# One layer's tokens taken past attention in two chunks, the expert gather of the first issued while the second is still in dense work

## The reference, cut to what matters

```
h = rmsnorm(x, norm1_g) * (1 + sc1) + sh1
f_in, c_in, q/k/v ..., gl = split(h @ w_in)
y_f, y_c, y_a, y_w = four mixers, each @ its output weights
gates = sigmoid(gl + b_gate)
merged = g0 * y_f + g1 * y_c + g2 * y_a + g3 * y_w
x = x + g1 * (merged @ w_out)
h = rmsnorm(x, norm2_g) * (1 + sc2) + sh2
q = (h @ w_q) as 8 heads x 2 halves of 128;  scores = q . subkeys (128 keys)
per head: top 16 of each half -> 256 pairs -> top 16 pairs -> 16 expert numbers
act = gelu(u[e] . h);  x = x + g2 * sum over 128 slots (softmax gate * act) * v[e]
```

## Time and profile before

| | |
|---|---|
| runs | 6071.48, 6000.5, 6046.06 us |
| profiled execution | 6077.76 us, its span 6075.9 us |
| mean granted TensorE clock | 0.873 |
| busy share of the span | PE 78%, PEld 44%, DVE 59%, ACT 14%, POOL 26% |
| DMA | 1509.71 MB, of which 1342.26 MB by the indirect gathers |
| last chain by engine | PE 47%, DMA 37%, DVE 10%, ACT 3% |

### The profile page before, as it was taken

How to read it: one execution, slowest core, us unless ns; L and a number is a source line. 1 busy time by engine, 2 the same in 40 slices (tenths; PEclk the granted TensorE clock), 3 DMA queues, 4 the chain that set the end, 5 groups by cost and what they waited for, 6 DMA issues and landing times.

```text
span 6075.9 us, 45921 instructions
## 1 busy us (share of the span) xinstructions
PE 4730.4 (78%) x14848; PEld 2693.3 (44%) x14848; DVE 3560.2 (59%) x7774; ACT 849.0 (14%) x2368; POOL 1566.3 (26%) x1310
## 2 busy tenths in 40 slices
PE   5989999896666666666679899998966666666665
PEld 3766677762222222222248566777722222222222
DVE  0655211158888888876419333111488888888765
ACT  1023200101111111111011322001011111111111
POOL 0000000004444454445200000000044444454453
PEclk7989999998888888888799669999988888888887
DMA  5100011119999999999730000111099999999997
GB/s 233 56 28 1 30 59 64 49 47 422 420 408 421 407 421 412 422 420 421 315 151 28 28 1 22 63 60 58 28 389 421 410 421 413 421 412 421 421 421 291
DMA packets 213696, 1509.71 MB, mean 248 GB/s; under 512 B 24656, under 2 KB 26960, under 8 KB 37072
## 3 DMA queue, kind: packets, MB, share of 16 engines
q0 software_dynamic: 184320, 1342.26, 53.3%
q1 hardware_dynamic: 29136, 164.52, 7.4%
HBM read 1503.54 MB, written 3.15 MB: 248 GB/s over the span
## 4 chain that ended last, share of the span: by engine, by line
PE 47%; DMA 37%; DVE 10%; ACT 3%; issue 2%; POOL 1%; DVEq 1%; SPq 0%; POOLq 0%; ACTq 0%
DMA B<-tables,R 21%; PE ps L625 9%; DMA A<-tables,R 8%; PE ps L702 7%; DMA R<-tables,R 6%; PE ps L465 5%; PE ps L630 5%; PE ps L682 4%; DVE B L1234 3%; DVE hT L1266 3%; PE ps L450 2%; PE ps L644 2%; PE ps L562 2%; PE ps L549 2%; DMA B<-ws 2%
## 5 line engine op out<-in xcount | busy, mean ns | idle before, releaser
L702 PE MATMUL ps<-B,hT 128*128 128x512 f32 x2752 | 1593.7, 730 | 768.8 <-ACT hT L897 768.8
L392 POOL DMA_INDIRECT B<-tables,R x908 | 1098.2, 1209 | 2784.7 <-DVE A L1223 1599.1
L702 PEld LDWEIGHTS ps<-B,hT 128*128 128x128 f32 x2752 | 623.6, 234 | 1706.6 <-ACT hT L897 932.5
L1234 DVE SCALAR_TENSOR_TENSOR B<-B,M 128x1024 f32<-128x1024 f32 x908 | 1096.1, 1224 | 319.7 <-DMA B<-tables,R 294.6
L702 PE MATMUL ps<-A,hT 128*128 128x512 f32 x864 | 528.8, 748 | 265.8 <-ACT hT L897 265.8
L625 PE MATMUL ps<-hT,B 128*128 128x320 f32 x2048 | 561.9, 432 | 1.4 <-ACT R L856 1.4
L625 PEld LDWEIGHTS ps<-hT,B 128*128 128x128 f32 x2048 | 389.0, 190 | 164.9 <-ACT R L856 3.0
L702 PEld LDWEIGHTS ps<-A,hT 128*128 128x128 f32 x864 | 198.6, 239 | 570.7 <-ACT hT L897 323.5
L392 POOL DMA_INDIRECT A<-tables,R x272 | 334.2, 1229 | 350.6 <-PE ps L702 268.2
L891 ACT ACTIVATE T<-T 128x4 f32<-128x4 f32 x320 | 65.7, 205 | 2413.6 <-DVEq L1236 2413.6
L1234 DVE SCALAR_TENSOR_TENSOR A<-A,M 128x1024 f32<-128x1024 f32 x272 | 332.8, 1225 | 116.9 <-DMA A<-tables,R 108.0
(11 more groups left out here) (205 smaller groups left out, 4695.8 us busy)
## 6 DMA issues: line engine op xcount, KB each, us to landing
B<-ws SPq DMA_DIRECT2D x96, 1024.0 KB, 4.9
B<-ws SPq DMA_DIRECT2D x64, 768.0 KB, 4.1
B<-tables,R POOLq DMA_INDIRECT x908, 17.9
R<-tabs SPq DMA_DIRECT2D x2, 2176.0 KB, 8.3
A<-tables,R POOLq DMA_INDIRECT x272, 20.4
x<-xin SPq DMA_DIRECT2D x1, 2560.0 KB, 9.2
y<-M SPq DMA_DIRECT2D x1, 2560.0 KB, 7.9
R<-tables,R POOLq DMA_INDIRECT x100, 18.4
```

The source lines that it names most:

```text
L392: pool.indirect_dma_start(out=ring[HOME[n]], out_offset=None, in_=tables[:, :], in_offset=bass.IndirectOffsetOnAxis(ap=EI[:, n:n + 1], axi ...
L702: mm = pe.matmul(ps[:, bk + c, :], diag[p % DIAGS], v_row[:, c * 512:(c + 1) * 512], start=(gt == 0 and i == 0), stop=(gt == GROUPS - 1 an ...
L1234: v.scalar_tensor_tensor(out=u_row, in0=u_row, scalar=1.0, in1=h2[:, n // SLOTS, :], op0=ALU.mult, op1=ALU.mult, accum_out=dots[:, n % (2 ...
```

## The change

From the merge on, tokens go in two chunks: tiles 0 and 1 (256 tokens), then tiles 2, 3 and 4 (384). The first chunk goes through merge, output projection, norm, queries and the selection for tile 0 alone. Then TensorE, ScalarE and VectorE interleave the second chunk's merge, projection, norm and queries with the expert work of tiles 0 and 1, by a fixed list in each engine. Those tiles' slots go in groups of 2 (before: 4). Of the two sums of a group one is TensorE's and one VectorE's up to slot 163; from slot 164 to 255, which is from the second chunk's queries on, both are TensorE's. Tiles 2 to 4 keep groups of 4 with three sums on TensorE. All 44 weight blocks past attention are loaded a second time. The ring starts with 6 homes, has 7 from slot 132, 12 from slot 236 and at last 15. The sigmoid becomes a tanh of half the argument, with the factors of one half put into a bias and into the row that scales the residual. In the front of the layer, halves of 512 and 128 columns become 256 and 384.

```diff
+CHUNKS = ((0, 1), (2, 3, 4))
-RING = 10
-NG = 4
+RING = 6
+GROUPS = [Group(t, n, size, size if 164 <= n < 2 * SLOTS else size // 2 + size // 4) for t in range(TILES) for size in ((2, 4)[CHUNK[t]],)
+          for n in range(t * SLOTS, (t + 1) * SLOTS, size)]
+LATER = {132: (6,), 236: (7, 8, 9, 10, 11), 352: (12,), 400: (13,), 528: (14,)}
...
 # GpSimd
-                pool.wait_ge(pq_s.sem, pq_s.at(l, UNITS))
+                    elif s == 3:
+                        pool.wait_ge(pq_s.sem, pq_s.at(l, UNITS))
+                    elif s == 7:
+                        pool.wait_ge(pq_s.sem, pq_s.at(l, 2 * UNITS))
...
 # TensorE, after the first chunk
+                for s in range(N_MG):
+                    mix_gates(l, 1, s)
+                    experts(l, s * MG_STEP)
+                    mix_branch(l, 1, s)
+                    experts(l, s * MG_STEP + 1)
+                for i in range(len(CHUNKS[1])):
+                    for part in range(4):
+                        out_part(l, 1, i, part)
+                        experts(l, AT_OUT + i * OUT_STEP + part)
+                for i, t in enumerate(CHUNKS[1]):
+                    experts(l, AT_NORM + i)
+                    norm_transposes(l, t, TILES + t, XSc[1][i % 2], i % 2 * 2, TILES + t - 2 if i >= 2 else None)
+                for i in range(len(CHUNKS[1])):
+                    row_transposes(l, 1, i)
+                    experts(l, AT_ROWS + i)
+                for hp in range(UNITS):
+                    queries(l, 1, hp)
+                    experts(l, AT_KEYS + hp * KEY_STEP)
+                    if hp:
+                        key_scores(l, 1, hp - 1)
+                    experts(l, AT_KEYS + hp * KEY_STEP + 1)
+                key_scores(l, 1, UNITS - 1)
+                for q in range(AT_END, N_GROUPS):
+                    experts(l, q)
...
 # ScalarE, after the first chunk
+                for s in range(N_MG):
+                    experts(l, s * MG_STEP)
+                    sigmoid(l, 1, s)
+                    experts(l, s * MG_STEP + 1)
...
+                for hp in range(UNITS):
+                    experts(l, AT_KEYS + hp * KEY_STEP)
+                    query_copy(l, 1, hp)
+                    experts(l, AT_KEYS + hp * KEY_STEP + 1)
...
 # VectorE
+                def experts(q):
+                    g = GROUPS[q]
+                    products(q)
+                    if g.tile and g.place == len(g.slots):
+                        residual(g.tile - 1)
+                    if q:
+                        sums(q - 1)
+                    if g.place == 0:
+                        gates(g.tile)
+                    weights(q)
...
+                for s in range(N_MG):
+                    if s:
+                        mix(1, s - 1)
+                    experts(s * MG_STEP)
+                    experts(s * MG_STEP + 1)
+                    select(1, s)
...
+                for hp in range(UNITS):
+                    experts(AT_KEYS + hp * KEY_STEP)
+                    if hp:
+                        score_copy(1, hp - 1)
+                        v.drain()
+                    if hp >= 2:
+                        select(2, hp * KEY_STEP - 4)
+                    experts(AT_KEYS + hp * KEY_STEP + 1)
+                    if hp >= 2:
+                        select(2, hp * KEY_STEP - 3)
+                score_copy(1, UNITS - 1)
+                v.drain()
+                for i in range(UNITS * KEY_STEP - 4, 4 * PH):
+                    select(2, i)
+                for q in range(AT_END, N_GROUPS):
+                    experts(q)
```

More of the change, by code:

```diff
@@ new lines, in norm_transposes, with experts @@
+            def norm_transposes(l, t, at, xs, bk, free):
+                pe.wait_ge(n_xs.sem, n_xs.at(l, at + 1))
+                if free is not None:
+                    pe.wait_ge(n_ht.sem, n_ht.at(l, free + 1))
+                for k in range(KD):
+                    last = pe.transpose(ps[:, bk + k // 4, (k % 4) * P:(k % 4 + 1) * P], xs[:, k * P:(k + 1) * P], ident)
+                last.then_inc(n_tp.sem, 1)
+            def experts(l, q):
+                g = GROUPS[q]
+                bk = 4 + (g.tile % 2) * 2
+                if g.place == 0 and g.tile >= 2:
+                    pe.wait_ge(tile_done.sem, tile_done.at(l, g.tile - 1))
+                for n in g.pe:
+                    v_row = ring[HOME[n]][:, D:ROW]
+                    pe.wait_ge(diag_ok.sem, diag_ok.at(l, PE_AT[n] + 1))
+                    for c in range(2):
+                        mm = pe.matmul(ps[:, bk + c, :], diag[PE_AT[n] % DIAGS], v_row[:, c * 512:(c + 1) * 512],
+                                       start=(n % SLOTS == 0), stop=(PE_AT[n] + 1 == PE_BY[g.tile]))
+                    mm.then_inc(pe_used.sem, 1)
@@ new lines, in out_part @@
+            def out_part(l, c, i, part):
+                n = AT_OP + c * AGAIN + part
+                bk, w, t = i % 2 * 2, home(n), CHUNKS[c][i]
+                if i == 0:
+                    arrived(l, n)
+                if part == 0 and i >= 2:
+                    pe.wait_ge(op_x.sem, op_x.at(l, t - 1))
+                for k in range(KD):
+                    last = pe.matmul(ps[:, bk + part // 2, (part % 2) * 256:(part % 2 + 1) * 256], mTc[c][:, k, i * P:(i + 1) * P],
+                                     w[:, k * 256:(k + 1) * 256], start=(k == 0), stop=(k == KD - 1))
+                if t == CHUNKS[c][-1]:
+                    last.then_inc(w_used.sem, 1)
+                elif part == 3:
+                    last.then_inc(op_ps.sem, 1)
@@ new lines, in _ @@
+                pe.wait_ge(mg_m.sem, mg_m.at(l, 2 * KD))
+                for i in range(len(CHUNKS[1])):
+                    for part in range(4):
+                        out_part(l, 1, i, part)
[6 more added lines that the diff above has]
+                    experts(l, AT_ROWS + i)
@@ new lines, in sums @@
+                def sums(q):
+                    g = GROUPS[q]
+                    for n in g.dve:
+                        v_row, o = ring[HOME[n]][:, D:ROW], n % (2 * SLOTS)
+                        if g.place == 0:
+                            last = v.tensor_scalar(out=acc, in0=v_row, scalar1=wgt[:, o:o + 1], scalar2=None, op0=ALU.mult)
+                        else:
+                            v.wait_ge(dve_used.sem, dve_used.at(l, DVE_AT[n]))
+                            last = v.scalar_tensor_tensor(out=acc, in0=v_row, scalar=wgt[:, o:o + 1], in1=acc, op0=ALU.mult,
+                                                          op1=ALU.add)
@@ new lines, in _ @@
+                for s in range(N_MG):
+                    if s:
[3 more added lines that the diff above has]
+                    select(1, s)
+                mix(1, N_MG - 1)
+                for i in range(len(CHUNKS[1])):
+                    for part in range(OUT_STEP):
+                        experts(AT_OUT + i * OUT_STEP + part)
+                    mixed(1, i)
+                means(n_ssq)
+                experts(AT_NORM)
@@ L1297, in _ @@
+                score_copy(1, UNITS - 1)
+                v.drain()
+                for i in range(UNITS * KEY_STEP - 4, 4 * PH):
+                    select(2, i)
+                for q in range(AT_END, N_GROUPS):
+                    experts(q)
+                    g = GROUPS[q]
+                    if g.tile in (2, 3):
+                        select(g.tile + 1, g.place // 4)
+                sums(N_GROUPS - 1)
+                residual(TILES - 1)
                 v.drain().then_inc(layer_done.sem, 1)
```

664 lines of the change are left out of this document (346 added, 318 removed).

## The result

| | before | after |
|---|---|---|
| median of the runs | 6023.28 us (5997.41 to 6071.48, 4 runs) | 6277.57 us (6250.91 to 6297.74, 4 runs) |
| ratio | | 1.041, interval 1.0319 to 1.0501 |
| profiled execution | 6077.76 us | 6295.67 us |
| mean granted TensorE clock | 0.873 | 0.831 |

The change makes the kernel 4% slower. The forecast was 5870 us with a range of 5730 to 6050, so the sign was wrong too.

What follows compares the result with a forecast made beforehand. Each layer was taken as a stretch bound by TensorE, then one bound by the gather; overlapping them gives 316 + 865 + 1049 = 2230 us against 2318.9. Saving 177 us from 6046 gives 5870 us, range 5730 to 6050.

Steps and rivals of the forecast that it cites:

- The other column split in the front of the layer moves the same columns: Ahead of the merge: halves of 256 and 384 columns for 512 and 128 were costed at nothing.
- The rival on the clock (3): TensorE's clock drops in second merge, projection and queries: 145 us a layer, time 6160 us; chance 0.08.
- The first chunk alone: From the merge's start to the first expert product: 316 us against 689.0, so 373 us earlier.
- The second merge: Second chunk's merge beside 128 slots: 12.3 us a step, 394 us, with VectorE, DMA and TensorE within 5%.
- Projection, norm and rows: Second chunk after its merge: projection 75 us (64 to 90), norm and rows 45 us (35 to 55).
- Queries: Second chunk's queries, 32 groups: VectorE and TensorE wait for each other, 21.7 us for 4 slots, 333 us.
- The ring: Second chunk's queries: VectorE's and TensorE's lists each wait for the other's later work, costing 125 us.
- Rival (1): Second queries: VectorE runs ahead, so no mutual wait; stage 208 us, time 5620 us; chance 0.12.
- The rest: After the second queries' groups: 18 us of selection parts and last scores, then 1049 us to the layer's end.
- Rival (2), six homes: Second merge: six homes don't cover the gather's landing; gain gone at 15.1 us a step, 6395 us at 20.5; chance 0.10.
- Rival (4), tables: Second merge: ScalarE switches tables twice a step, 6 us a layer; at twice the cost 90, time 6050 us; chance 0.05.
- The sum: Merge to layer end: 316 + 865 + 1049 = 2230 us against 2318.9, 88 us a layer, 177 in all.

Runs made afterwards that it cites:

- the six and the eight matmuls: Unread matmuls: six ahead of each latent tile's query transposes, changed kernel 6133.84 us, kernel before 6317.57; eight ahead of the first latent tile, kernel before, 6163.65.
- a_load: Changed kernel with the second merge's first four weight blocks loaded earlier, no longer each waiting for the block just before it: median 6128.31 us.
- a_order: Changed kernel with VectorE taking both groups of a unit before the copy of the scores in the second queries: median 5996.35 us.
- a_best: Changed kernel with the earlier loads of the second merge's first four blocks and VectorE's both-groups-first order in the second queries together: 5847.06 us, ratio 0.9633.
- a_fill: Changed kernel with only unread matmuls in attention, one behind each windowed unit's scores and two behind a tile's query transposes: 6025.95 us, ratio 0.9982.

## Why the prediction was wrong, step by step

**The step that failed** is "The other column split in the front of the layer moves the same columns": I costed by columns what had to be costed by its effect on the waits of TensorE behind it, and took the stretch before the merge as given. In its place the runs showed attention at half clock: 250.6 us more in the two layers, 121 of them with the column split alone. My windows began at 678, where attention ends. Had I asked for the same windows of layer 1, I would have seen attention 81 us longer there (347.4 against 266.7), with the same code, in the one trace that I had, with granted clock 0.50 in two of its tiles:

```profile
3440.00:3470.00 30.00, 30.00 (x98) 19.61 (x97) 10.04 (x31) 6.66 (x20) 0.00 (x0) 0.50 0.00 1
...
3620.00:3650.00 30.00, 30.00 (x180) 20.88 (x181) 18.59 (x58) 12.51 (x38) 0.00 (x0) 1.00 0.01 1
```

The rival on the clock (3) looked for the loss in the new merge, where the clock is 0.96 to 0.99; it had the right kind of loss in the wrong place. The Trainium skill (TensorE: Matmul & The Clock Gate, "A second HAM failure mode: psum-queue depth-cycling") says that short idles between groups of matmuls can make the clock oscillate; the trace agrees in that waits of 1.35 us go with a fall, but they recur only once a tile, the same wait stands in tiles that keep the clock, and the half clock lasts for the rest of the tile, some 92 of 95 us.

What is shown: attention makes the whole loss, the column split alone makes about half of it, a filled wait takes it away in all eight tiles. Open is why a given shift gives a given tile its duration; the six and the eight matmuls changed it in ways that I can't derive. The forecast had 0.16 on slower, in part for "what I have not seen"; no rival named this stretch.

A second miss lies past the merge and would have stood without attention: the two layers took 67 and 94 us more than the 2230 forecast, 52 of each in the second merge. Two slips in the working are small: the first chunk's terms add up to 315, not 316, and the plateaus of the earlier trace rows go down to 407 GB/s, not 408.

**The first chunk alone**: right, 317.8 and 319.9 us for 316.

**The second merge**: mechanism right (three engines near full, DMA the first), size wrong: 446 for 394 us. Of the 52 us, a_load's 24 to 28 are the first loads' wait for the block just before them. I had seen that wait at the projection's weights, given it 2 us, and none at the merge's. Some 25 more are the mixed DMA traffic: I divided the reloads' bytes by 421 GB/s and got 12.0 as the lower bound. Without the reloads the step is 12.18, near what VectorE's list (11.8) and TensorE's (11.4) gave; TensorE is then the fullest engine, 275.43 of 293 us.

**Projection, norm and rows**: 128.3 and 127.2 for 120, inside the bounds.

**Queries**: right. The unit shown takes 21.1 us for 21.7, the stage 344.2 for 333, DMA at 210 GB/s in the window above as forecast, and VectorE idle until TensorE's scores. The ring costs 115 us a layer by a_order; the sum had 125. Rival (1) has it that the ring does not close; it closes, and one moved line opens it. That the second sum sits in the ring was priced with 2.4 net; it is 48 us over 16 units, 3.0 each.

**The rest**: 1060.6 us in layer 0 for 18 + 1049 = 1067; with queries 1404.8 for 1400, where two small errors partly cancel.

**Rival (2), six homes**: not at its price, but it wasn't nothing. Its sign was 15.1 us a step for the gain to be gone, and more idle of VectorE ending in DMA. The later steps take 13.11 us; VectorE waits 10.5 + 9.8 + 8.0 = 28 us for rows in 341 us of the second merge, by the view of the gathers' line, and the run without reloads has 5.7 us. The rows land late beside the reloads, by some 1 us a step.

**Rival (4), tables**: no. Groups of table loads in the changed kernel: ten at the softmax's exponential, twelve at the gelu; the tanh at L825 has none, so it shares the gelu's table. The Trainium skill (ScalarE: Activation LUTs, "Table sets") lists tanh with exp and with sigmoid, and calls gelu_apprx_tanh separate from gelu, not from tanh. It doesn't say whether tanh and gelu_apprx_tanh share a table; these rows show the two without a load between them.

```profile
L854 ACT ACT_TABLE_LOAD x12 | 15.4, 1283 | 0.2
L851 ACT ACT_TABLE_LOAD x10 | 12.8, 1283 | 0.2
```

**The sum**: 88 us a layer forecast past the merge, 22 and 15 measured; with the two mendings 160 and 154 (a_best: 2319.0 - 2159.0 and 2339.2 - 2185.3). So the first version of the change gains a quarter of the forecast or less past the merge, and the mended one more. The forecast took the ring as given, though; without its 125 us it would have been 213, and by that measure 160 is less than the idea seemed to offer.

## What to carry to other kernels

Before you cost a change at nothing in a stretch, look at that stretch's granted clock in every layer: if the same code has two durations in one trace at two granted clocks, a shift elsewhere may turn it, as the column split, the six matmuls and the eight did here. Look for the wait that comes at the same place in each unit of work, and fill it with work that nobody reads: two matmuls a tile took the two attentions here from 347.5 and 388.4 to 278.4 and 269.7 us. Compare variants only with that held, or their stages one by one; the four runs of a_order alone lie 166 us apart (5859.11 to 6025.06), while its queries' stage is 229.7 and 229.0 us in the two layers.

In lists that interleave two pipelines, write down for each engine what the other waits for. If both lists put the first group's sums, then the scores, then the second group, the two chains add up; issuing both groups first gave back what the ring took.

## What the runs showed of the hardware

- The kernel before ran in steps of 31 to 37 us: its 13 runs beside the last experiments lie at 5998 to 6006, 6032 to 6040, 6068 to 6078, and one at 6105, with mean granted clocks of 0.883 to 0.887, 0.879 to 0.881, 0.875 to 0.876 and 0.869. That such a spread counts tiles at half clock (40.4 us each) fits this, but only runs of the third heap were profiled.
- The mean granted clock can be 0.53 over a 428.8 us stage, at 1.2 GHz for 92 of each 95 us tile, with TensorE shown busy 30.00 of 30 us. With nothing added but matmuls that nobody reads it was 0.94 over that stage (a_fill, 297.6 us).
- Weight loads of 768 KB among the gathers bring the DMA engines to 376 GB/s at a share of 0.96; the gather alone moves 421 at 1.01. Without the loads the same steps moved 345 at 0.91.
